# Layer 2's input turned by VectorE squares and a DRAM exchange instead of TensorE transposes; latent weights loaded two tiles' loads later

## What is computed

```python
(r_q, r_k, r_v, a_cq, a_ckv, a_kpe, l_x, l_v, l_o, l_i, l_f, c_q, z) = _split_cols(x @ w_in, IN_SPLITS)
...
memo = _merge(_mem_attention(c_q, mem, w_mem_kv)).astype(f32)
y = jnp.concatenate([ret, mla, mls, memo], axis=-1) * jax.nn.silu(z.astype(f32))
y = y.astype(x.dtype) @ w_out
return _layernorm(DEEPNORM_ALPHA * x + y, ln_g, ln_b)
```

## Time and profile before

| | us |
|---|---|
| median of 3 runs | 906.46 |
| the profiled execution | 907.26 |
| its span | 905.4 |
| TensorE busy | 899.3 (99%) |
| VectorE busy | 654.7 (72%) |
| ScalarE busy | 493.6 (55%) |
| granted TensorE clock, mean | 0.999 |

### The profile page before, as it was taken

How to read it: one execution, slowest core, us unless ns; L and a number is a source line. 1 busy time by engine, 2 the same in 40 slices (tenths; PEclk the granted TensorE clock), 3 DMA queues, 4 the chain that set the end, 5 groups by cost and what they waited for, 6 DMA issues and landing times.

```text
span 905.4 us, 13911 instructions
## 1 busy us (share of the span) xinstructions
PE 899.3 (99%) x4872; PEld 781.5 (86%) x4872; DVE 654.7 (72%) x1294; ACT 493.6 (55%) x934; POOL 16.0 (2%) x18
## 2 busy tenths in 40 slices
PE   9999999999999999999999999999999999999997
PEld 8888998888888888888888889888888888888896
DVE  6868776877775775666669787778777667787865
ACT  6665765645545455644476657746354544555551
POOL 0000000000000000000000000000000000000001
PEclk9999999999999999999999999999999999999999
DMA  9785456645874475656654865585475754766832
GB/s 358 270 320 163 133 173 232 186 142 176 276 250 162 162 225 197 206 187 196 199 187 140 306 222 157 174 245 165 137 232 163 232 166 162 231 189 233 338 102 93
DMA packets 58132, 183.03 MB, mean 202 GB/s; under 512 B 6856, under 2 KB 12240, under 8 KB 57424
## 3 DMA queue, kind: packets, MB, share of 16 engines
q1 hardware_dynamic: 57488, 181.10, 61.0%
q10 hardware_dynamic: 576, 1.05, 0.3%
HBM read 174.78 MB, written 7.35 MB: 201 GB/s over the span
## 4 chain that ended last, share of the span: by engine, by line
PE 98%; issue 1%; DMA 0%; ACT 0%; POOL 0%; DVE 0%; POOLq 0%; ACTq 0%; DVEq 0%
PE acc L1330 23%; PE acc L1315 18%; PE acc L1316 18%; PE acc L1319 18%; PE acc L1336 12%; PE work L1044 1%; PE work L1051 1%; PE work L1050 1%; PE work L1049 1%; PE work L1214 1%; PE work L1213 1%; DMA B<-in_mem_t 0%; PE work L1242 0%; PE work L1230 0%; PE work L1145 0%
## 5 line engine op out<-in xcount | busy, mean ns | idle before, releaser
L1402 DVE TENSOR_TENSOR lo<-raw,hi 128x512 fp32r<-128x512 f32 (+2 forms) x607 | 387.6, 657 | 204.3 <-ACT hi L1008 190.9
L1008 ACT ACTIVATE hi<-raw 128x512 fp32r<-128x512 f32 (+2 forms) x607 | 351.4, 603 | 270.0 <-PE acc L1319 143.1
L1315 PE MATMUL acc<-hi,xx 128*128 128x512 f32 (+2 forms) x576 | 213.4, 374 | 0.0
L1316 PE MATMUL acc<-hi,xx 128*128 128x512 f32 (+2 forms) x576 | 209.0, 366 | 0.0
L1330 PE MATMUL acc<-xx,hi 128*128 128x512 f32 x768 | 193.5, 394 | 0.0
L1319 PE MATMUL acc<-lo,xx 128*128 128x512 f32 (+2 forms) x576 | 164.3, 366 | 0.0
L1330 PEld LDWEIGHTS acc<-xx,hi 128*128 128x128 f32 x768 | 138.2, 189 | 24.9
L1316 PEld LDWEIGHTS acc<-hi,xx 128*128 128x128 f32 x576 | 108.6, 189 | 16.0
L1315 PEld LDWEIGHTS acc<-hi,xx 128*128 128x128 f32 x576 | 108.6, 189 | 16.1
L1319 PEld LDWEIGHTS acc<-lo,xx 128*128 128x128 f32 x576 | 104.3, 188 | 17.7 <-DVE lo L1402 0.3
L1336 PEld LDWEIGHTS acc<-xx,lo 128*128 128x128 f32 x768 | 104.8, 190 | 7.6
(11 more groups left out here) (347 smaller groups left out, 1041.1 us busy)
## 6 DMA issues: line engine op xcount, KB each, us to landing
raw<-in_w SPq DMA_DIRECT2D x263, 512.0 KB, 3.9
raw<-in_w SPq DMA_DIRECT2D x26, 256.0 KB, 2.7
raw<-in_w SPq DMA_DIRECT2D x16, 328.0 KB, 3.1
B<-turn SPq DMA_DIRECT2D x40, 128.0 KB, 3.7
turn<-B SPq DMA_DIRECT2D x6, 512.0 KB, 5.5
Y<-in_wuq SPq DMA_DIRECT2D x2, 1152.0 KB, 7.4
Y<-in_x_t SPq DMA_DIRECT2D x4, 512.0 KB, 9.0
X<-in_x SPq DMA_DIRECT2D x4, 512.0 KB, 6.5
```

The source lines that it names most:

```text
L1008: act.activation(place(l, t, hi), raw[:, s, (t % 2) * w:(t % 2 + 1) * w], ACT.Copy)\
L1315: pe.matmul(o, ah[:, q], hi[:, s, 0:w], start=k == 0, stop=False, skip_group_check=name == "memv")
L1316: pe.matmul(o, al[:, q], hi[:, s, 0:w], start=False, stop=False, skip_group_check=name == "memv")
L1402: dve.tensor_tensor(place(l, t, lo), raw[:, s, (t % 2) * w:(t % 2 + 1) * w], place(l, t, hi).bitcast(F32), ALU.subtract).then_inc(lo_done. ...
```

## The change

Layer 1's input is no longer turned by TensorE. A new VectorE step `turn_x` transposes the 32x32 blocks of four feature blocks (a group) into `squares`, behind slots 10, 13, 16 and 19. SyncE writes group g to DRAM at m = 9, 11, 13, 15 and issues its four returns, to Y, at m = 12, 14, 16, 18. `x_hi` and `x_lo` read the returned group in Y through `turned_block` and no longer a bank of PSUM, and stand in pairs: ScalarE at slots 22, 23, 26, 27, 30, 31, 34, 35, VectorE a slot later. The latent weights, which overwrite Y, are loaded at m = 24 in both layers and wait for the last `x_lo`. The gain step loses its wait for the last `xT`. The arithmetic is the same.

```diff
--- before.py
+++ after.py
@@ -131,8 +131,11 @@
     table.setdefault(slot, []).append(step)
 
 
-for _j in range(8):
-    _put(LATER_PE, 16 + 2 * _j, "xT", _j)
+for _g in range(4):
+    _put(LATER_DVE, 10 + 3 * _g, "turn_x", _g)
+    for _n in range(2):
+        _put(LATER_ACT, 22 + 4 * _g + _n, "x_hi", 2 * _g + _n)
+        _put(LATER_DVE, 23 + 4 * _g + _n, "x_lo", 2 * _g + _n)
 for _h in range(HEADS):
     _put(PE_AT, (71, 75, 81, 87)[_h], "mem_scores", _h)
     _put(PE_AT, (78, 84, 91, 98)[_h], "mem_pT", _h)
@@ -157,7 +160,6 @@
 ACT_AT = {}
 for _j in range(8):
     _put(LATER_ACT, 8 + 3 * _j // 2, "normalise", _j)
-    _put(LATER_ACT, 21 + 2 * _j, "x_hi", _j)
     _put(FIRST_ACT, 15 + 2 * _j, "x_hi", _j)
     if _j:
         _put(FIRST_ACT, 2 * _j - 1, "m_hi", _j + 1)
@@ -191,7 +193,6 @@
 
 DVE_AT = {}
 for _j in range(8):
-    _put(LATER_DVE, 21 + 2 * _j, "x_lo", _j)
     _put(FIRST_DVE, 16 + 2 * _j, "x_lo", _j)
     _put(FIRST_DVE, 22 + 2 * _j, "angles", _j)
     if _j > 2:
@@ -235,7 +236,8 @@
         (244, "y_lo", 4), (245, "y_lo", 5), (251, "y_lo", 6), (252, "y_lo", 7)]:
     _put(DVE_AT, _s, *_step)
 
-TURNS = ("c", "cell", "rq", "rk", "ret")
+TURNS = ("c", "cell", "rq", "rk", "ret", "x0", "x1", "x2", "x3")
+X_OUT_AT, X_IN_AT = {9: 0, 11: 1, 13: 2, 15: 3}, {12: 0, 14: 1, 16: 2, 18: 3}
 TURN_OUT_AT = {57: "c", 77: "cell", 81: "rq", 89: "rk", 112: "ret"}
 TURN_IN_AT = {59: "c", 79: "cell", 83: "rq", 91: "rk", 114: "ret"}
 
@@ -420,6 +422,9 @@
                    "ret": B[7][:, 0:1024]}
         turn_to = {"c": B[7][:, 0:1024], "cell": B[5][:, 0:1024], "rq": B[0][:, 0:1024], "rk": B[8][:, 0:1024],
                    "ret": B[8][:, 0:1024]}
+
+        for g in range(4):
+            squares[f"x{g}"], turn_to[f"x{g}"] = B[2 + g][:, 0:1024], Y[:, g * 1024:(g + 1) * 1024]
 
         def turned_block(name, j):
 
@@ -671,12 +676,8 @@
                     if m == 20:
                         sp.dma_start(B[6][:, 0:1024], a["lw"][l:l + 1, :].rearrange("o (p n) -> p (o n)", p=P))\
                           .then_inc(lw_in.sem, 16)
-                    if m == 22:
-
-                        if l == 0:
-                            sp.wait_ge(x_lo.sem, x_lo.at(0, 7))
-                        else:
-                            sp.wait_ge(y_lo.sem, y_lo.at(l - 1, 7))
+                    if m == 24:
+                        sp.wait_ge(x_lo.sem, x_lo.at(l, 7))
                         sp.dma_start(Y[:, 0:1024], a["wukv"][l:l + 1, :].rearrange("o (p n) -> p (o n)", p=P))\
                           .then_inc(mlaw_in.sem, 16)
                         sp.dma_start(Y[:, 1024:3328], a["wuq"][l:l + 1, :].rearrange("o (p n) -> p (o n)", p=P))\
@@ -696,6 +697,18 @@
                         wait_job(sp, l, ("mem_out", 1))
                         sp.dma_start(B[9][:, 0:1024], a["mrow"].rearrange("h t -> (h t)").partition_broadcast(P))\
                           .then_inc(mrow_in.sem, 16)
+                    if l and m in X_OUT_AT:
+                        name = f"x{X_OUT_AT[m]}"
+                        sp.wait_ge(squared[name].sem, 1)
+                        sp.dma_start(a["turn"][TURNS.index(name)], squares[name]).then_inc(turn_out[name].sem, 16)
+                    if l and m in X_IN_AT:
+                        name = f"x{X_IN_AT[m]}"
+                        sp.wait_ge(turn_out[name].sem, 16)
+                        sp.wait_ge(y_lo.sem, y_lo.at(0, 7))
+                        for b in range(4):
+                            sp.dma_start(turn_to[name][b * 32:(b + 1) * 32, :].rearrange("c (a n) -> c a n", a=4),
+                                         a["turn"][TURNS.index(name), :, b * 256:(b + 1) * 256]
+                                         .rearrange("(a c) n -> c a n", a=4)).then_inc(turn_in[name].sem, 16)
                     if m in TURN_OUT_AT:
                         name = TURN_OUT_AT[m]
                         sp.wait_ge(squared[name].sem, squared[name].at(l, 0))
@@ -809,10 +822,11 @@
                         act.activation(xh[:, 2 * j:2 * j + 2, :], xT0[:, j, :].rearrange("p (k t) -> p k t", k=2),
                                        ACT.Copy).then_inc(x_hi.sem, 1)
                         return
-                    wait_job(act, l, ("xT", j))
+                    act.wait_ge(turn_in[f"x{j // 2}"].sem, 64)
                     act.wait_ge(cols_in.sem, cols_in.at(l, 0))
                     for k in (2 * j, 2 * j + 1):
-                        m = act.activation(xh[:, k, :], bank(l, ("xT", j))[:, (k % 2) * 256:(k % 2 + 1) * 256], ACT.Identity,
+                        m = act.activation(xh[:, k, :].rearrange("p (i a r) -> p i a r", i=NT, a=4),
+                                           turned_block(f"x{j // 2}", k % 4), ACT.Identity,
                                            scale=cols[:, C_LNG + k:C_LNG + k + 1], bias=cols[:, C_LNB + k:C_LNB + k + 1])
                     m.then_inc(x_hi.sem, 1)
 
@@ -1053,16 +1067,6 @@
                 def both(parts, at):
                     return tuple(at(x) for x in parts)
 
-                def xT(j):
-                    pe.wait_ge(ident_in.sem, 16)
-                    pe.wait_ge(normed.sem, 2 * (j // 2) + 2)
-                    o = take("xT", j)
-                    for kk in range(2):
-                        for i in range(NT):
-                            m = turn(o[:, kk * 256 + i * P:kk * 256 + (i + 1) * P],
-                                     X[:, i, (2 * j + kk) * P:(2 * j + kk + 1) * P])
-                    m.then_inc(job_done.sem, 1)
-
                 def mem_scores(h):
                     if h == 0:
                         pe.wait_ge(kq_split.sem, kq_split.at(l, 3))
@@ -1254,7 +1258,7 @@
                         m = pe.matmul(o[:, c + P:c + 256], pt[:, 2 * P:3 * P], rv[:, 1, v], start=False, stop=True)
                     m.then_inc(job_done.sem, 1)
 
-                steps = {"xT": xT, "mem_scores": mem_scores, "mem_pT": mem_pT, "mem_out": mem_out,
+                steps = {"mem_scores": mem_scores, "mem_pT": mem_pT, "mem_out": mem_out,
                          "ml_fold": ml_fold, "ml_q": ml_q, "gateT": gateT,
                          "gate_cols": gate_cols, "kpeT": kpeT,
                          "ml_scores": ml_scores, "ml_out": ml_out, "mla_qr": mla_qr, "mla_kn": mla_kn,
@@ -1451,12 +1455,12 @@
                     if l:
                         dve.wait_ge(cols_in.sem, cols_in.at(l, 0))
                         for k in (2 * j, 2 * j + 1):
-                            m = dve.tensor_scalar(tmp[:, (k % 2) * 256:(k % 2 + 1) * 256],
-                                                  bank(l, ("xT", j))[:, (k % 2) * 256:(k % 2 + 1) * 256],
+                            m = dve.tensor_scalar(tmp[:, (k % 2) * 256:(k % 2 + 1) * 256]
+                                                  .rearrange("p (i a r) -> p i a r", i=NT, a=4),
+                                                  turned_block(f"x{j // 2}", k % 4),
                                                   cols[:, C_LNG + k:C_LNG + k + 1], cols[:, C_LNB + k:C_LNB + k + 1],
                                                   ALU.mult, ALU.add)
-                        m.then_inc(free_bank(l, "xT", j), 1)
-                        wait_read(dve, l, ("xT", j))
+                        link(m)
                         src = tmp[:, :].rearrange("p (k t) -> p k t", k=2)
                     dve.tensor_tensor(xl[:, 2 * j:2 * j + 2, :], src, part, ALU.subtract).then_inc(x_lo.sem, 1)
                     if l:
@@ -1467,7 +1471,6 @@
                     blk = X[:, i, cb * 512:(cb + 1) * 512]
                     if b == 0:
                         dve.wait_ge(gb0_in.sem, 16)
-                        wait_job(dve, l, ("xT", 7))
                     link(dve.tensor_tensor(blk, blk, gb0[:, 0, cb * 512:(cb + 1) * 512], ALU.mult))
 
                 def offset(b):
@@ -1541,6 +1544,14 @@
                                 m.then_inc(conv_done.sem, 1)
                             else:
                                 link(m)
+
+                def turn_x(g):
+
+                    dve.wait_ge(normed.sem, 2 * g + 2)
+                    for i in range(NT):
+                        m = dve.transpose(squares[f"x{g}"].rearrange("p (b i j r) -> p i j b r", b=4, i=NT, j=4)[:, i],
+                                          X[:, i, g * 512:(g + 1) * 512].rearrange("p (j b c) -> p j b c", j=4, b=4))
+                    m.then_inc(squared[f"x{g}"].sem, 1)
 
                 def rms_(r):
                     dve.wait_ge(sq_done.sem, sq_done.at(l, r))
@@ -1824,7 +1835,7 @@
                 steps = {"angles": angles_, "lo": lo_of, "x_lo": x_lo_, "m_lo": m_lo, "gain": gain, "offset": offset, "kept_lo": kept_lo_, "y_lo": y_lo_, "memv": memv, "mem_max": mem_max, "mem_norm": mem_norm,
                          "mem_out": out_pair("mem_out", memo), "conv": conv, "rms": rms_, "ckv": ckv, "cqn": cqn_,
                          "kpe_rope": kpe_rope, "gates": gates, "gate_scan": gate_scan, "skip": skip, "ones": ones,
```

(2 more changed lines are left out.)

## The result

The changed kernel takes **908.32 us** (median of 9 runs), the kernel before 906.16 beside it. The ratio is 1.003, with a 95% interval of 1.0021 to 1.0039: slower by about 0.3%, 2.2 us, where 903.8 was forecast. It is inside no case of the forecast but rival (c). One of the nine runs took 5125 us, for a reason that is not known; it is left out of the ratio, and without it the median is 908.1. The profiled execution took 910.14 us, its span 908.3.

A forecast was written before the change was run, and what follows sets the result against it. TensorE was taken as the bound, VectorE just behind. -3.55 + 0.6 + 0.3 = -2.65 us on the profiled 907.26 gave 904.6; with the runs' median 0.8 lower, the forecast was 903.8, range 902.8 to 907.4.

The forecast's parts named there:

- rival (c): Late exchange holds ScalarE's x_hi of groups 0 and 2, slowing the kernel; 8 us per return gives 908.4; chance 0.13.
- Transposes, -3.55 us: TensorE in layer 1: removing eight turning steps of 0.44 us from the chain saves 3.55 us.
- rival (d): TensorE's 32 transposes cost their full duration of 0.272 us each: net -7.8 us, 898.7; chance 0.01.
- `turn_x` 1.3 us: VectorE: each of four added transpose steps takes 1.3 us; three are absorbed by idle time.
- `x_lo` 1.37 us: VectorE: scalings through the turned view 0.65 plus subtraction 0.72 give 1.37 us per step, upper 1.75.
- rival (b): VectorE becomes the bound: turned view costs the old 1.03, or returns take 6.7 us; about 906; chance 0.33.
- Step 1: Exchange of group 0: returns are in 5.7 us after first issue, bounds 4.1 and 10.0; VectorE just fits.
- Step 2: Slots 23 to 25: slot 25's split ends at 481.85; group 2's return is issued at 482.3, in at 488.0.
- Groups 1 and 3 are not later by the same count: Returns of groups 1 and 3, between groups 0 and 2, were counted as no later than those.
- The stall of +0.6 us: TensorE at slot 39: its tile is ready at 502.8, wanted at 502.2, a stall of 0.6 us.
- Latent weights, +0.3 us: Near cq's end in layer 1: later wukv and wuq loads cost 0.3 us, bounds 0 and 1.1.
- Layer 0, priced at nothing: Layer 0: the same move of the latent weights is covered and costs nothing; the +0.3's upper end covers it.

The follow-up runs named there:

- experiment 6: Changed kernel, but x_hi and x_lo do not wait for the returns (wrong result) and wuq's splits stand behind the convolution: 903.41 us.
- experiment 7: Changed kernel with x's returns in 4 KB packets, quadrants in the wrong order: 908.73 us.
- 9: Kernel of experiment 5 with the sixteen returns issued from GpSimd's queue instead of SyncE's: 903.78 us.
- 15: Kernel of experiments 10 without the exchange's writes; returns read one block written in the first layer (wrong result): 902.63 us.
- experiment 16: Kernel of experiments 10 with one return of 128 partitions per group, in the wrong layout: 902.13 us.
- experiment 13: Changed kernel with only the returns issued ahead of the ring's wait and the weight load: 903.76 us.
- 17: Kernel of experiments 10 with four writes of 32 partitions and one return of 128 per group, complete: 902.47 us.
- experiment 2: Changed kernel with x's writes and returns left out, reading the unexchanged squares (wrong result): 903.9 us.
- experiments 1: Changed kernel, but x_hi and x_lo read the squares without waiting for the returns, transfers still run (wrong result): 903.96 us.
- 3: Kernel before the change with only the latent weights' loads moved from m = 22 to m = 24: 905.43 us.
- 18: Changed kernel with only four writes of 32 partitions and one return of 128 per group: 905.47 us.
- experiments 10: Kernel of experiment 5 with the returns issued ahead of the ring's wait and the weight load: 903.2 us.
- experiment 5: Changed kernel with the query weights' (wuq) splits moved behind the convolution: 907.77 us.

## Why the prediction was wrong

Rival (c) happened, at the place and through the mechanism that it named (ScalarE's `x_hi` ahead of a tile, TensorE idle for `hi`, 2.71 us before slot 30), with its own sign of over 3 us of wait. It had a chance of 0.13. Its price for 8 us per return, 908.4, beside the measured 908.3, is in part luck: it is +1.95 us, where the stretch grew by 3.96 and the medians differ by 2.2, and the latent weights' larger cost and the 1.13 us ahead of the stretch are not in it. By the steps of the text:

- *Transposes, -3.55 us*: right. The stretch lost 3.5 us of turning steps, 0.44 each, and rival (d)'s price by duration was rightly left out.
- *`turn_x` 1.3 us*: right, 1.30, and covered.
- *`x_lo` 1.37 us*: 1.50 (0.77 and 0.73 from start to start). The pair of scalings through the turned view takes 0.77 against the lower bound of 0.65. `x_hi` takes 1.00 per pair from start to start, 0.93 was taken. Small, and rival (b)'s turned view at the old cost did not occur: with nothing waiting for the returns (experiment 6) the stretch stood only 0.40 us over the pairs.
- ***Step 1, "a group is in 5.7 us after its first issue": this failed, by its size.*** It took 8.3, 8.9, 7.5 and 6.9. The 5.7 was a fair reading of the kernel before, whose ten exchange groups took 4.9 to 6.7 us. But the engines were less busy around them: over 24 us, the share was 0.65 to 0.91 there and 0.99 in the change (466 to 490). The text wrote 4 MB of exchange off against free tenths of the DMA engines and did not add up how busy they would be: in three windows the share went from 0.52, 0.29 and 0.59 to 1.03, 1.01 and 1.01. Weight loads landed later there too, 5.2 to 7.6 us after their issue for 3.3 to 4.0 before. Full engines alone do not explain the length: two groups of the kernel before had a share of 0.98 in their first 6 us (from 262.5 and 334.3) and took 5.3 and 5.6. It is not the packets' size (experiment 7), the queue (9) or the writes (15), and the one return of experiment 16 takes off 2.1 us, mostly issues. The rest of the cause stays open.
- *Step 2, the issue moments*: right in kind. The text issues group 2's returns behind slot 25's split, which stands behind both `x_lo` of group 0, and says that lateness counts at group 0 and again at group 2. So it was. Counted from the entry into the stretch, group 0 landed 2.4 us later than forecast, slot 25's split ended and group 2's issue came 2.7 later, and group 2 landed 4.5 later. What the text did not ask is whether the order itself could be otherwise: experiment 13 has groups of 7.1 to 8.7 us and is at 903.76. That this is the forecast 903.8 is chance.
- *"Groups 1 and 3 are not later by the same count"*: both came late. Group 1 took longest, 8.9 us, and made a standstill of its own (0.88 at slot 24). Group 0 cost 0.21 directly, though ScalarE waited 3.08 us for it; through group 2's issue it had its part in the largest (2.87 at slot 28).
- *The stall of +0.6 us*: without waits for Y the count gives nothing, and 0.38 to 0.39 at slot 36 is left (experiments 6, 16, 17), the `x_lo` steps being 0.13 longer each than priced. In the change, 1.54 stood at slots 32 to 38, besides 4.10 at 20 to 30.
- *Latent weights, +0.3 us*: 1.86 at slots 46 to 62. The landing was mis-sized here too: 9.5 us after its issue where 7.8 was taken. It is not the late VectorE or the exchange that makes the cost. VectorE stood idle for 4.09 us before its first step of `wuq`, and experiment 2, with no exchange at all, has the same landing (9.5) and the same loss (1.79). Over six profiles the loss follows the landing: `wuq` in 0.1, 0.2, 0.7, 0.8, 1.5 and 1.6 us after the start of slot 46's pair, and 0.36, 0.53, 1.04, 1.13, 1.79 and 1.86 us lost (experiments 1, 3, 13, 18, 2, the change). What makes one landing 8.0 us and another 9.5 stays open.
- *Layer 0, priced at nothing*: the changed kernel's profile loses 0.8 us there, between 150 and 175 us, and others between 0 and 1.3. The cause was not looked for.

The count that the text left out: 0.5 MB written and 0.5 MB back in two pairs of tiles, 5.6 us, beside two weight loads, are 2.1 MB, about 375 GB/s. In the changed kernel the full engines moved 258 to 291 in the three windows above, and at most 360 with returns in flight in any window of 6 us read here, though at the kernel's start loads alone reach 406 GB/s over 24 us. With this count rival (c) would have deserved a larger chance.

## What to carry to other kernels

Before adding a round trip through DRAM, add up what the DMA engines have to move in the windows where it runs, not over the span. If it will keep them full for long, take landings longer than those of short bursts: here 4.9 to 6.7 us per group became 6.9 to 8.9. Put the issue of a return ahead of any wait that a stall of its reader can delay; otherwise one late transfer makes a later one late. When quadrants or blocks are exchanged, bring the data back in one DMA over all partitions and let the write be the one in parts: the return is what an engine waits for, and each issue saved is some 0.5 us of it.

## What the runs showed of the hardware

**The form of the landing side.** Loads and returns alone (experiment 15: the returns on 32 partitions each, all from one block of DRAM) kept the engines full at 241 GB/s, 71 ns per KB; with 128-partition returns they moved 354 GB/s at 44 ns per KB (experiment 16), and four DMAs that read 32 partitions each left them at 46 (experiment 17). With writes running beside the 32-partition returns it is 56 in the change and 47 in experiment 13, so the stretching depends on what else is in flight, and a cost of the 32-partition form alone is not isolated. Of the 2.1 us that one return instead of four takes off a group, 1.6 are the three issues saved (experiments 10 and 16). Packets of 4 KB do not help (experiment 7).
The Trainium skill (SBUF — State Buffer, Door 1: The DMA port swizzle) says that a transfer over partitions 0 to 31 reaches 8 of 16 ports, that 0 to 63 reaches the same 8, and that this halves its bandwidth. Experiment 15 agrees in direction, with 71 against 44 to 49 ns per KB over all traffic, if its single block of DRAM has no part in it; experiment 13, with 47, shows no such cost. The writes of experiment 17, which read 32 partitions each, show none either (46).

**Another queue is not another road.** Sixteen returns issued by GpSimd landed no sooner after their issue (7.8 to 9.8 us per group) than those of SyncE (5.8 to 9.5 in experiment 5). A queue of its own buys the moment of issue, and that was worth 4 us here.
